# Feed-forward of a hybrid decoder trunk: unit 4 of six becomes a unit of seven block products, so that three such units follow each other

## The chip, the cores and the metric

The kernel runs on one core of one Trainium2 chip. Its time is the device time of one execution in microseconds (us); lower is better. TensorE (PE in the profile) multiplies, VectorE (DVE) and ScalarE (ACT) work element by element, GpSimd (POOL) here issues a few DMAs and small operations, SyncE (SP) issues the plain DMAs.

## What is computed

A trunk of four layers over 256 tokens of width 1024. Each layer is a feed-forward, a token mixer (attention, SSD, short convolution, attention in turn) and a second feed-forward; so there are eight feed-forwards. The change touches these alone:

```python
def swiglu(x, w_gu, w_down):          # x 256 x 1024, w_gu 1024 x 5632, w_down 2816 x 1024
    gate, up = jnp.split(x @ w_gu, 2, axis=-1)
    return (jax.nn.silu(gate) * up) @ w_down

for i in range(DEPTH):                # DEPTH = 4
    x = x + 0.5 * swiglu(rmsnorm(x, ffn1_norm[i]), ffn1_w_gu[i], ffn1_w_down[i])
    x = x + mixer_i(rmsnorm(x, mix_norm[i]))
    x = x + 0.5 * swiglu(rmsnorm(x, ffn2_norm[i]), ffn2_w_gu[i], ffn2_w_down[i])
```

## The kernel before

**Weights.** All weights are float32 and pass through the core once. A weight block is 512 x 512 (or 256 x 1024) numbers, 1 MB, as a tile of 128 x 2048. It is loaded by DMA into one of six staging slots (`stage`; slots 3 to 5 lie in the `arena`, so their rows show that name), then split in two: ScalarE copies it, rounded, into `w_hi` (line 721), VectorE subtracts that from the block and writes the rest into `w_lo` (line 1067). There are three pairs of `w_hi` and `w_lo`, used in turn: ScalarE may fill a pair once TensorE has ended the block three before. TensorE then makes each product in three passes, high by high, high by low and low by high, with matmuls of 512 columns.

**Units.** A feed-forward goes over the 2816 hidden columns in six units, u = 0 to 5, whose kinds the string `UNITS` (line 51) gives. A plain unit `P` takes 512 hidden columns, that is four weight blocks, G0, G1 (gate) and U0, U1 (up), each multiplied with both halves of the tokens: 24 matmuls a block, 96 in all, in banks 4, 5 and 6, 7. `H` is a plain unit of 256 columns with two blocks, H0 and H1. `S` also takes 512 columns, but by the scheme of seven products: gate, up, the two halves of the 1024 inputs and the two halves of the tokens make a 2 x 2 by 2 x 2 block product, which needs seven block products instead of eight when sums of blocks are multiplied. They are B11, A1, B22, A3, B21, A2, A4, each with 12 matmuls (line 1633), 84 in all. B blocks come as they are loaded; A blocks are sums of weight blocks:

- A1: VectorE adds block B12 to B11 in B11's slot (`weight_sum`, line 1178). It does so before ScalarE can split A1.
- A3: GpSimd issues an accumulating DMA that adds B22 to B12's slot (line 660), once the sum for A1 is done.
- A2: a second accumulating DMA adds B22 to B11's slot (line 663), once A1's low part is done.
- A4: VectorE adds that slot to B21's (line 1178), once the second DMA has landed.

The results of the products overlap in banks 4 to 7, and gate and up come out of them by sums: ScalarE copies three banks to SBUF (line 784), VectorE makes five part sums (line 1151), ScalarE the silu of two (line 780) and VectorE the product with up (line 1147). TensorE transposes the hidden into banks 6 and 7 (line 1667), which are split into `mt_hi` (ScalarE, line 790) and `mt_lo` (VectorE, line 1157). Then come the down blocks of the unit, D0 and D1, 24 matmuls each (line 1520).

**Order.** `ffn_order` writes out the order of all blocks of a feed-forward; `DOWNS` says how many waiting down blocks go into each unit. Before the change it is, with the unit's number: 0: G0 G1 U0 U1. 1: B11 A1 B22 D0(0) D1(0) A3 B21 A2 A4. 2: H0 H1 D0(1). 3: B11 A1 D1(1) B22 D0(2) A3 B21 A2 A4. 4: G0 G1 D0(3) U0 U1 D1(3). 5: B11 A1 B22 D0(4) A3 B21 A2 A4 D1(4) D0(5) D1(5). A unit's transposes follow the first two products, or the first block, of the next.

Every engine works its own list in order, made from this one. ScalarE and VectorE split the block that is two ahead: at step i they do first what TensorE's block i-1 released (copies, part sums), then the split of block i+2, and where block i+2 is B11, VectorE then makes the sum for A1; where it is B21, the sum for A4. Before the first block of a unit that follows an `S` unit, TensorE waits until bank 4 is copied and the third part sum has read bank 5:

```python
                    else:
                        pe.wait_ge(part_copied, 3 * sums_before(f, u))
                        pe.wait_ge(part_summed, 5 * sums_before(f, u) - 2)
```

Loads are issued by SyncE in order, each as soon as the slot's last user is split; a planner gives each load the slot that is free first.

Of the kernel before, what the change touches and what calls it, by code (L numbers as in the profile page):

```python
# [47 lines left out]
SSD_STAGE_SLOTS = 3  # L48


UNITS = "PSHSPS"
DOWNS = (0, 2, 1, 2, 2, 1)


def unit_col(u):

    return sum(256 if kind == "H" else 512 for kind in UNITS[:u])


def down_parts(u):  # L60

    return 1 if UNITS[u] == "H" else 2


def ffn_order():

    order, turned, waiting = [], {}, []
    for u, kind in enumerate(UNITS):
        own = {"P": ("G0", "G1", "U0", "U1"), "H": ("H0", "H1"),
               "S": ("B11", "A1", "B22", "A3", "B21", "A2", "A4")}[kind]  # L70
        own = [(u, name) for name in own]
        lead, head = {"P": (1, 2), "H": (1, 2), "S": (2, 3)}[kind]
        if u:
            waiting += [(u - 1, f"D{j}") for j in range(down_parts(u - 1))]
        now, waiting = waiting[:DOWNS[u]], waiting[DOWNS[u]:]
        order += own[:lead]
        if u:
            turned[u - 1] = len(order) - 1
        if kind == "S" and UNITS[u - 1] == "H":
            order += now[:1]  # L80
            now = now[1:]
        order += own[lead:head]
        if kind == "P":
            order += now[:1] + own[2:] + now[1:]
        else:
            order += now + own[head:]
    turned[u] = len(order) - 1
    return order + waiting + [(u, f"D{j}") for j in range(down_parts(u))], turned


FFN_ORDER, TURNED_AFTER = ffn_order()
N_UNITS, N_SUMS = len(UNITS), UNITS.count("S")
HOME = {"A1": "B11", "A2": "B11", "A3": "B12", "A4": "B21"}
# [13 lines left out]
def build_trunk(nc, x, ffn1_norm, ffn1_w_gu, ffn1_w_down, mix_norm, ffn2_norm, ffn2_w_gu,  # L107
# [149 lines left out]
    def sums_before(f, u):  # L257

        return N_SUMS * f + UNITS[:u].count("S")

# [1842 lines left out]
```

## Time and profile before

| | |
|---|---|
| median of 3 runs | 2031.96 us (2031.28 to 2492.7) |
| profiled execution | 2032.11 us, span of its instructions 2030.4 us |
| TensorE busy | 2000.0 us, 99% of the span, 10299 matmuls |
| VectorE busy | 1566.5 us, 77% |
| ScalarE busy | 1185.2 us, 58% |
| GpSimd busy | 166.4 us, 8% |
| DMA | 419.87 MB, mean 207 GB/s |
| granted TensorE clock | 0.999 |

The busy times are of one profiled execution. A matmul's own duration (0.39 us for 512 columns) overlaps the next one's; what a block takes is read from start to start. The feed-forward that is looked at most closely is the third of eight (the first of layer 1), at about 504 to 684 us.

### The profile page before, as it was taken

What the parts mean: (1) busy time and instruction counts of PE and PEld (TensorE: products, weight loads), DVE (VectorE), ACT (ScalarE), POOL (GpSimd) and SP (SyncE); (2) the same over time, 40 slices, a digit from 0 to 9 for tenths busy, and PEclk for the clock granted to TensorE, in tenths of its full rate; (3) what the DMA queues carried; (4) which work ended last, traced back from release to release, by engine and by line L of the source; (5) the groups of instructions that cost most, each with busy time, mean ns of one, the idle gap of its engine ahead of it and who ended that gap; (6) DMA issues with size and microseconds to landing.
All of it is one profiled execution on the core that took longest, in us unless ns stands there. A gap on an engine that the chain in (4) does not pass through costs nothing.

```text
span 2030.4 us, 25272 instructions
## 1 busy us (share of the span) xinstructions
PE 2000.0 (99%) x10299; PEld 1705.7 (84%) x10299; DVE 1566.5 (77%) x1485; ACT 1185.2 (58%) x1263; POOL 166.4 (8%) x164
## 2 busy tenths in 40 slices
PE   7999999999999999999999999999999999999998
PEld 6888997888888889988888888988888888998886
DVE  6778577878887879968878778778778778567776
ACT  6556576556665666756556556446555546576544
POOL 1000001000000014410001000000001001001000
PEclk9999999999999999999999999999999999999999
DMA  8867534877787485368876867658876867534863
GB/s 268 254 230 228 185 104 129 246 247 228 224 251 210 138 263 141 125 226 237 243 218 192 250 231 194 204 190 247 243 227 190 256 214 232 166 121 129 260 223 108
DMA packets 242183, 419.87 MB, mean 207 GB/s; under 512 B 10668, under 2 KB 92932, under 8 KB 241556
## 3 DMA queue, kind: packets, MB, share of 16 engines
q1 hardware_dynamic: 216020, 363.65, 52.9%
q0 software_dynamic: 26048, 54.61, 14.9%
q8 instruction: 82, 1.34, 0.3%
q14 instruction: 33, 0.27, 0.0%
HBM read 417.14 MB, written 1.08 MB: 206 GB/s over the span
## 4 chain that ended last, share of the span: by engine, by line
PE 87%; DVE 7%; ACT 3%; issue 1%; DMA 1%; POOL 0%; SPq 0%; DVEq 0%; POOLq 0%; ACTq 0%
PE bank L1520 51%; PE bank L1633 22%; PE bank L1526 7%; DVE w_lo L1067 3%; PE bank L1667 2%; DVE arena L1387 2%; ACT w_hi L721 2%; PE bank L1553 1%; PE bank L1804 1%; PE bank L1835 1%; DMA stage<-in_ffn_w_gu 0%; PE bank L1817 0%; ACT arena L965 0%; DMA arena<-seg_rows 0%; DVE arena L1427 0%
## 5 line engine op out<-in xcount | busy, mean ns | idle before, releaser
L1067 DVE TENSOR_TENSOR w_lo<-stage,w_hi 128x2048 fp32r<-128x2048 f32 (+1 forms) x225 | 517.0, 2299 | 161.4 <-ACT w_hi L721 160.2
L1067 DVE TENSOR_TENSOR w_lo<-arena,w_hi 128x2048 fp32r<-128x2048 f32 (+1 forms) x196 | 444.3, 2267 | 167.5 <-ACT w_hi L721 166.7
L721 ACT ACTIVATE w_hi<-stage 128x2048 fp32r<-128x2048 f32 (+1 forms) x225 | 425.4, 1892 | 216.6 <-PE bank L1520 143.0
L721 ACT ACTIVATE w_hi<-arena 128x2048 fp32r<-128x2048 f32 (+1 forms) x196 | 371.9, 1898 | 241.3 <-PE bank L1520 160.0
L1520 PE MATMUL bank<-w_hi,mt_hi 128*128 128x512 f32 x928 | 367.4, 396 | 5.2 <-DVE mt_lo L1274 3.8
L1520 PE MATMUL bank<-w_lo,mt_hi 128*128 128x512 f32 x928 | 361.5, 390 | 0.0
L1520 PE MATMUL bank<-w_hi,mt_lo 128*128 128x512 f32 x928 | 360.9, 390 | 0.0
L1520 PE MATMUL bank<-w_hi,xt_hi 128*128 128x512 f32 x704 | 279.7, 397 | 2.1 <-DVE w_lo L1067 1.6
L1520 PE MATMUL bank<-w_lo,xt_hi 128*128 128x512 f32 x704 | 275.7, 392 | 0.0
L1520 PE MATMUL bank<-w_hi,xt_lo 128*128 128x512 f32 x704 | 251.7, 390 | 0.0
L1520 PEld LDWEIGHTS bank<-w_hi,mt_hi 128*128 128x128 f32 x928 | 174.4, 188 | 40.3 <-DVE mt_lo L1274 4.2
L1520 PEld LDWEIGHTS bank<-w_hi,mt_lo 128*128 128x128 f32 x928 | 174.2, 188 | 37.0
L1526 PE MATMUL bank<-xt_hi,w_hi 128*128 128x256 f32 x704 | 203.4, 290 | 1.2 <-DVE arena L1387 0.7
L1520 PEld LDWEIGHTS bank<-w_lo,mt_hi 128*128 128x128 f32 x928 | 174.5, 188 | 34.4
L1526 PE MATMUL bank<-xt_hi,w_lo 128*128 128x256 f32 x704 | 198.1, 283 | 0.0
L1526 PE MATMUL bank<-xt_lo,w_hi 128*128 128x256 f32 x704 | 195.4, 283 | 0.0
L1520 PEld LDWEIGHTS bank<-w_hi,xt_hi 128*128 128x128 f32 x704 | 132.9, 189 | 32.5 <-issue 3.9
L1520 PEld LDWEIGHTS bank<-w_hi,xt_lo 128*128 128x128 f32 x704 | 132.2, 188 | 28.0
L1520 PEld LDWEIGHTS bank<-w_lo,xt_hi 128*128 128x128 f32 x704 | 132.9, 189 | 26.2
L1633 PE MATMUL bank<-w_hi,mt_hi 128*128 128x512 f32 x384 | 151.1, 393 | 0.1
L1633 PE MATMUL bank<-w_hi,mt_lo 128*128 128x512 f32 x384 | 149.7, 390 | 0.0
L1633 PE MATMUL bank<-w_lo,mt_hi 128*128 128x512 f32 x384 | 149.5, 389 | 0.0
(213 smaller groups left out, 2802.8 us busy)
## 6 DMA issues: line engine op xcount, KB each, us to landing
arena<-in_ffn_w_gu SPq DMA_DIRECT2D x81, 1024.0 KB, 5.3
stage<-in_ffn_w_gu SPq DMA_DIRECT2D x79, 1024.0 KB, 5.2
stage<-in_ffn_w_down SPq DMA_DIRECT2D x96, 512.0 KB, 4.9
arena<-in_ffn_w_down SPq DMA_DIRECT2D x80, 512.0 KB, 4.9
arena<-in_ffn_w_gu POOLq DMA_DIRECT2D x29, 1024.0 KB, 9.8
stage<-in_ffn_w_gu POOLq DMA_DIRECT2D x19, 1024.0 KB, 9.8
stage<-in_ffn_w_gu SPq DMA_DIRECT2D x18, 512.0 KB, 8.8
stage<-in_sb_w_qkv SPq DMA_DIRECT2D x16, 512.0 KB, 4.6
```

The costliest lines, as they stand in the source:

```text
L721: act.activation(w_hi[q][:, 0:c], stage[s][:, 0:c], ACT.Copy).then_inc(hi_done, 1)
L1067: dve.tensor_tensor(w_lo[q][:, 0:c], stage[s][:, 0:c], w_hi[q][:, 0:c].bitcast(F32), ALU.subtract).then_inc(lo_done, 1)
L1387: dve.scalar_tensor_tensor(chan[:, c, i:SEQ], bank[c][:, 0:SEQ - i], par[:, t:t + 1], chan[:, c, i:SEQ], ALU.mult, ALU.add).then_inc(tap_d ...
L1520: mm = pe.matmul(out_, x_[a], w[b], start=start and (a, b) == (0, 0), stop=stop and (a, b) == (1, 0))
L1526: mm = pe.matmul(out_, w[b], x_[a], start=start and (a, b) == (0, 0), stop=stop and (a, b) == (1, 0), skip_group_check=True)
L1553: mm = pe.transpose(tb[i % 2][:, k * P:(k + 1) * P], xk, ident[:, :])
L1633: mm = pe.matmul(out_[:, :], x[a], w[b], start=start and k == 0 and (a, b) == (0, 0), stop=stop and k == 3 and (a, b) == (1, 0), skip_grou ...
L1667: mm = pe.transpose(tb[b][:, c * SEQ + h * P:c * SEQ + (h + 1) * P], hid[:, h, col:col + P], ident[:, :])
L1804: pe.matmul(z[:, 0:SEQ], kk[:, 0:P], qq, start=True, stop=True, skip_group_check=True)
L1835: pe.matmul(o[:, 0:SEQ], v(0), w[:, 0:SEQ], start=h % 2 == 0, stop=True, skip_group_check=True)
```

## The change

The string of the units gets an `S` in the place of its last `P`. Unit 4 is then one of seven products, and units 3, 4 and 5 are all of this kind.

```diff
--- before.py
+++ after.py
@@ -48,7 +48,7 @@
 SSD_STAGE_SLOTS = 3
 
 
-UNITS = "PSHSPS"
+UNITS = "PSHSSS"
 DOWNS = (0, 2, 1, 2, 2, 1)
```

The order of blocks in units 4 and 5 becomes: 4: B11 A1 B22 D0(3) D1(3) A3 B21 A2 A4. 5: as before. A feed-forward has 45 steps instead of 42; TensorE has 96 matmuls fewer over the whole program.

Below are VectorE's rows of the first feed-forward where unit 3 ends and unit 4 begins, from the part sum after A3 of unit 3 (line 1151, reading bank 6) on. Line 1067 is the low part of a weight block, line 1178 a weight sum. Before the change:

```order
L1151 TENSOR_TENSOR arena<-arena,bank 128x512 [waits part_copied,block_used]
L1067 TENSOR_TENSOR w_lo<-stage,w_hi 128x2048 [waits hi_done]
L1151 TENSOR_TENSOR arena<-bank,arena 128x512 [waits part_copied,block_used]
L1067 TENSOR_TENSOR w_lo<-arena,w_hi 128x2048 [waits hi_done]
L1151 TENSOR_TENSOR arena<-bank,arena 128x512 [waits part_copied]
L1151 TENSOR_TENSOR arena<-arena 128x512 [waits part_copied,part_summed]
L1067 TENSOR_TENSOR w_lo<-stage,w_hi 128x2048 [waits hi_done]
L1151 TENSOR_TENSOR arena<-bank,arena 128x512 [waits part_copied,block_used]
L1147 TENSOR_TENSOR arena<-arena 128x512 [waits part_summed,silu_done] x2
```

And after it:

```order
L1151 TENSOR_TENSOR arena<-arena,bank 128x512 [waits part_copied,block_used]
L1067 TENSOR_TENSOR w_lo<-stage,w_hi 128x2048 [waits hi_done]
L1151 TENSOR_TENSOR arena<-bank,arena 128x512 [waits part_copied,block_used]
L1067 TENSOR_TENSOR w_lo<-arena,w_hi 128x2048 [waits hi_done]
L1178 TENSOR_TENSOR arena<-stage,arena 128x2048 [waits stage_in0]
L1151 TENSOR_TENSOR arena<-bank,arena 128x512 [waits part_copied]
L1151 TENSOR_TENSOR arena<-arena 128x512 [waits part_copied,part_summed]
L1067 TENSOR_TENSOR w_lo<-arena,w_hi 128x2048 [waits hi_done]
L1151 TENSOR_TENSOR arena<-bank,arena 128x512 [waits part_copied,block_used]
L1147 TENSOR_TENSOR arena<-arena 128x512 [waits part_summed,silu_done] x2
```

The low part behind the second row of line 1151 is that of unit 4's first block (G0 before, B11 now). Behind it now stands the weight sum for A1 of unit 4, and only then the two part sums that follow A2 of unit 3, the first of which frees bank 5.

ScalarE's rows at the same place, from the high part of A4 of unit 3 on (line 721, waiting for w_summed), before:

```order
L721 ACTIVATE w_hi<-stage 128x2048 [waits block_used,w_summed]
L721 ACTIVATE w_hi<-arena 128x2048 [waits block_used,stage_in3]
L784 ACTIVATE arena<-bank 128x512 [waits block_used]
L721 ACTIVATE w_hi<-stage 128x2048 [waits block_used,stage_in0]
L780 ACTIVATE arena<-arena,rstd 128x512 [waits part_summed] x2
L721 ACTIVATE w_hi<-stage 128x2048 [waits block_used,stage_in1]
L790 ACTIVATE mt_hi<-bank 128x512 [waits ht_ps] x2
L721 ACTIVATE w_hi<-arena 128x2048 [waits block_used,stage_in4]
```

and after:

```order
L721 ACTIVATE w_hi<-stage 128x2048 [waits block_used,w_summed]
L721 ACTIVATE w_hi<-arena 128x2048 [waits block_used,stage_in3]
L784 ACTIVATE arena<-bank 128x512 [waits block_used]
L721 ACTIVATE w_hi<-arena 128x2048 [waits block_used,w_summed]
L780 ACTIVATE arena<-arena,rstd 128x512 [waits part_summed] x2
L721 ACTIVATE w_hi<-stage 128x2048 [waits block_used,stage_in1]
L784 ACTIVATE arena<-bank 128x512 [waits block_used]
L721 ACTIVATE w_hi<-arena 128x2048 [waits block_used,stage_in4]
L784 ACTIVATE arena<-bank 128x512 [waits block_used]
L790 ACTIVATE mt_hi<-bank 128x512 [waits ht_ps] x2
```

The second block of unit 4 (the row ahead of line 780) waited for its load and now waits for a weight sum, and the copies of line 784 for unit 4 stand between the high parts.

On TensorE the first matmul of unit 4 keeps its waits: for its low part, for the copy of bank 4 and for the third part sum of unit 3. It is now a product's matmul (line 1633), and 12 of them stand before the next block, where there were 24.

## Rows read from the trace of the kernel before

**Rows 1.** Page: engines' busy time, share and count; the chain that ended last

```profile
PE 2000.0 (99%) x10299; PEld 1705.7 (84%) x10299; DVE 1566.5 (77%) x1485; ACT 1185.2 (58%) x1263; POOL 166.4 (8%) x164
...
PE 87%; DVE 7%; ACT 3%; issue 1%; DMA 1%; POOL 0%; SPq 0%; DVEq 0%; POOLq 0%; ACTq 0%
```

**Rows 2.** Windows: length, busy us of PE, PEld, DVE, ACT, POOL; clock, DMA share, GB/s

```profile
605.60:648.50 42.90, 42.90 (x197) 35.53 (x197) 28.74 (x21) 22.42 (x19) 2.56 (x2) 1.00 0.75 208
```

**Rows 3.** TensorE's waits, whole run: total us, times, longest

```profile
PE bank L1520 <- DVE mt_lo L1274: 3.8, 2, 1.9
...
PE bank L1520 <- DVE w_lo L1067: 1.6, 1, 1.6
```

**Rows 4.** Timeline of VectorE: start, us, line, operation; end of unit 3

```profile
602.54 2.28 DVE L1067 TENSOR_TENSOR w_lo<-stage,w_hi 128x2048 fp32r<-128x2048 f32 x1
604.74 0.68 DVE L1151 TENSOR_TENSOR arena<-bank,arena 128x512 f32<-128x512 f32 x1
605.35 0.68 DVE L1151 TENSOR_TENSOR arena<-arena 128x512 f32<-128x512 f32 x1
```

**Rows 5.** Timeline of TensorE where unit 4 begins

```profile
605.61 0.44 PE L1520 MATMUL bank<-w_hi,xt_hi 128*128 128x512 f32 x1
```

**Rows 6.** Timeline of TensorE, unit 5: B11, A1, transposes, B22, D0(4), A3

```profile
639.28 0.39 PE L1633 MATMUL bank<-w_hi,xt_hi 128*128 128x512 f32 x1
...
642.00 0.39 PE L1633 MATMUL bank<-w_hi,mt_hi 128*128 128x512 f32 x1
...
644.72 1.03 PE L1667 MATMUL bank<-ident,arena 128*128 128x128 f32 x8
645.66 0.47 PE L1633 MATMUL bank<-w_hi,mt_hi 128*128 128x512 f32 x1
...
648.50 0.39 PE L1520 MATMUL bank<-w_hi,mt_hi 128*128 128x512 f32 x1
...
653.95 0.39 PE L1633 MATMUL bank<-w_hi,mt_hi 128*128 128x512 f32 x1
```

**Rows 7.** Timeline of all engines where TensorE waits for VectorE in attention

```profile
306.57 0.41 DVE L1274 TENSOR_TENSOR mt_lo<-bank,mt_hi 128x256 fp32r<-128x256 f32 x1
...
307.04 0.50 PE L1520 MATMUL bank<-w_hi,mt_hi 128*128 128x512 f32 x1 [1.91 <-DVE mt_lo L1274]
...
307.38 0.39 PE L1520 MATMUL bank<-w_lo,mt_hi 128*128 128x512 f32 x1
...
307.61 0.40 PE L1520 MATMUL bank<-w_hi,mt_lo 128*128 128x512 f32 x1
```

**Rows 8.** Timeline of all engines, A1 of unit 5: sum, high part, low part

```profile
632.82 2.29 DVE L1178 TENSOR_TENSOR stage<-stage 128x2048 f32<-128x2048 f32 x1
...
635.13 1.92 ACT L721 ACTIVATE w_hi<-stage 128x2048 fp32r<-128x2048 f32 x1 [4.56 <-DVE stage L1178]
635.39 1.28 POOL L660 DMA_DIRECT2D stage<-in_ffn_w_gu  x1 [57.82 <-DVE stage L1178]
637.09 2.29 DVE L1067 TENSOR_TENSOR w_lo<-stage,w_hi 128x2048 fp32r<-128x2048 f32 x1 [0.79 <-ACT w_hi L721]
```

**Rows 9.** Accumulating DMAs by line, from issue to landing: line 663, then line 660

```profile
DMA to landing us min/median/max: 9.7/10.5/13.2
...
DMA to landing us min/median/max: 8.5/8.7/9.8
```

**Rows 10.** Page: DMA queues, packets, MB, share of 16 engines

```profile
q1 hardware_dynamic: 216020, 363.65, 52.9%
q0 software_dynamic: 26048, 54.61, 14.9%
```

**Rows 11.** Timeline of TensorE in the first microseconds

```profile
12.71 1.11 PE L1553 MATMUL bank<-ident,x_res 128*128 128x128 f32 x4 [4.47 <-DMA x_res<-in_x]
...
16.43 0.63 PE L1520 MATMUL bank<-w_hi,xt_hi 128*128 128x512 f32 x1
16.86 0.63 PE L1520 MATMUL bank<-w_lo,xt_hi 128*128 128x512 f32 x1
```

## The prediction

> **What bounds the kernel now.** First the page's busy shares and its chain [rows 1]: TensorE is busy 99% of the span, VectorE 77%, and TensorE's own matmuls make 87% of the chain that ended last. The kernel is bound by TensorE nearly everywhere, so matmuls removed are worth their full price, provided that the feeders still arrive in time. The windows view [rows 2] shows that for the stretch that the change rewrites, in the third of eight feed-forwards: from 605.6 to 648.5 us TensorE is busy 42.90 of 42.90 us, VectorE 28.74, ScalarE 22.42, the DMA engines 75%. TensorE's waits [rows 3] hold one wait on a low part (w_lo) in the whole run, 1.6 us, at the start; no feed-forward stalls on its weights.
>
> Averages don't say how late the feeders are. For that I read VectorE's and ScalarE's timelines beside TensorE's, at the one place where a unit of seven products ends (unit 3; the units are numbered 0 to 5 as in the code). There the covers are thin. The third part sum of unit 3 runs 604.74 to 605.42 [rows 4], and the next unit's first matmul, which waits for it, starts at 605.61 [rows 5]: 0.19 us between them, with TensorE never idle. That wait is what the change meets.
>
> **What the change takes away.** Unit 4 turns from four blocks of 24 matmuls into seven of 12: 84 for 96. A product takes 2.72 us (639.28, 642.00, 644.72 [rows 6]), a down block 5.45 (648.50 to 653.95 [rows 6]). Today the stretch from unit 4's first matmul, 605.61, to the down block D0(4), 648.50, takes 42.89 us. Afterwards it holds, without any stall: B11, A1, transposes and B22 of unit 4, for which the same pieces of unit 5 stand, 648.50 - 639.28 = 9.22; two down blocks, 10.90; A3, B21, A2, A4, 4 x 2.72 = 10.88; and the 9.22 of unit 5. That is 40.22, so 2.67 us less in each feed-forward. With eight of them 21.4 us.
>
> **What it adds.** VectorE: three more low parts and two more weight sums, each 2.20 us from start to start (602.54 to 604.74), five part sums of 0.60 [rows 4], while ScalarE gets three more high parts and three copies for the two silus that it keeps. On average that fits: 5 x 2.20 + 5 x 0.60 = 14.0 us on top of 28.74 is 42.7, but of a stretch that now lasts 40.2 to 47 us. So VectorE goes from a third idle to nearly full, and what counts is the order in which it works. The order shows the new trouble: between the low part of unit 4's first block and the third part sum of unit 3 now stands the 2048-wide weight sum for A1 of unit 4. I carry the times forward from the rows, with t as in the trace.
>
> *First stall, B11.* VectorE starts the weight sum at 604.74, where the third part sum stood, and goes on 2.20 us later, at 606.94. The part sum ends 0.68 later, at 607.62. TensorE reacts to a VectorE result in 0.06 us (low part of mt ends 306.57 + 0.41 = 306.98, matmul at 307.04 [rows 7]), so B11 starts at 607.68: **2.07 us late**. Nothing hides it, since bank 4 and bank 5 still hold unit 3's results.
>
> *Second stall, A1.* Its weights exist only once summed: sum, then high part, then low part, in a chain. Today's A1 of unit 5 shows the links: sum 632.82 + 2.29, high part at 635.13, low part at 637.09 [rows 8]. There two blocks of 5.4 us stood ahead of B11 and TensorE reached A1 only at 642.00. In the new place: sum ends 604.74 + 2.29 = 607.03, high part 607.05 to 608.97, low part 609.01 to 611.30, TensorE 611.36. B11 ends at 607.68 + 2.72 + 0.12 = 610.52 (0.12: after a wait the first matmul takes 0.34 to the next instead of 0.23 [rows 7]). **0.84 us late**. Even without the first stall A1 would wait for this chain.
>
> *Third, B22.* After A1's low part is issued (611.22) VectorE has a part sum and two products of the hidden, 1.80 us, then B22's low part, 613.02 to 615.31, TensorE 615.37. TensorE would be there at 611.36 + 2.84 + 0.94 (transposes, 644.72 to 645.66) = 615.14. **0.23 us late**, B22 ends at 618.21. The low half of the hidden is ready at 615.23 + 2.21 + 0.68 = 618.12, so D0(3) does not wait. It would start at 605.61 + 9.22 = 614.83 without stalls: the transition costs **3.38 us**.
>
> *Again at unit 5.* The two down blocks (10.90 us) let VectorE catch up: it has two low parts, one more and a sum in them. So A3 to A4 of unit 4 run at the same margins as unit 3's, and the transition from 4 to 5 costs the same 3.38. This also delays the second added DMA of unit 5, whose issue follows A1's low part by 0.3 us: 645.7 + 0.3 = 646.0; with the median of 10.5 us to landing [rows 9] it is there by 656.5, and the sum for A4 may start as late as 658.9 before A2's low part misses TensorE at 663.5. The slots of the staging area are freed six or seven blocks ahead in the new order, as now, so the plain loads keep their lead.
>
> *Sum.* 2 x 3.38 - 2.67 = +4.09 us per feed-forward; eight times, **+32.7 us**. Outside the feed-forwards nothing changes but slot numbers. The profiled execution took 2032.11 us (span 2030.4), the median shown is 2031.96. So 2064.7, rounded to 2065 us, 1.6% slower.
>
> **Prices seen from one side only.** A stall's restart (0.12) may not be paid where it falls before a wait that VectorE sets anyway; it may be paid three more times per transition: 0 to +0.36 each, 0 to +6 us. Bank 4's part sum might be read with 0.19 instead of 0.06 us of delay: 0 to +2. The extra DMA traffic: the accumulating queue moved 54.61 MB in 14.9% of the span and the other 363.65 MB in 52.9% [rows 10], so the eight new units add 16 MB at 5.5 us per MB, 92 us of DMA time in all, hidden in a DMA that is 75% busy here, and free unless a landing comes late.
>
> **Rivals.**
> *The second added DMA lands too late.* 24 of them took 9.7 to 13.2 us [rows 9]; unit 5's limit is 658.9 - 646.0 = 12.9. At 14 to 15 each feed-forward loses 1 to 2 us more: 2073 to 2081. For it: it runs beside denser traffic and a denser VectorE. Against it: the same loads surround it today, and only the slowest exceeds the limit. The Trainium skill (SBUF: State Buffer, "SBUF: two separate sides") says that GpSimd's descriptors wait while VectorE works in a two-port mode. By that rule each issue could be late by one VectorE instruction, 2.3 us, which is 13.2 to landing and +0.3 us per feed-forward; the trace shows the first added DMA issued at 635.39 right behind a weight sum and beside further VectorE work [rows 8], and all 24 of its kind landed within 8.5 to 9.8 us [rows 9], a spread of 1.3. Chance 0.10.
>
> *TensorE's clock falls in the stalls.* The granted clock is 1.00 in this stretch [rows 2], the 2.4 GHz level. When TensorE had been idle 4.47 us at the start, its matmuls then came 0.43 us apart rather than 0.23 [rows 11], the 1.2 GHz level. The new stalls are 2.1 and 0.8 us. If each transition lost one product's time to it, 16 x 2.72 = 43 us: 2108. Against it: after 1.91 us of idle at 307.04 the spacing is 0.23 at once [rows 7]. The Trainium skill (TensorE: Matmul & The Clock Gate, "What's actually happening") has the same two levels and says that inactivity brings the lower one; by it, stalls that add up would cost this way. Chance 0.05.
>
> *No stalls: it is faster.* If the transitions hid their waits, 2032.1 - 21.4 = 2011. The averages speak for it (VectorE 77%), and it decides at 1.34 us per transition: under that the change gains. Against it stands the order: 2.20 us of sum before a wait with 0.19 us of slack. Chance 0.05.
>
> *Half of it.* The second and third stall vanish, because B11's stall gives the feeders time: 2 x 2.07 - 2.67 = 1.47, 2044. I computed them behind the first, so I give it 0.08.
>
> **The numbers.** The forecast, 2058 to 2072 on its own, has 0.72. With a late landing and part of the half case the range that leaves out 2 in 10 is 2050 to 2080. Two per cent, about what a measurement of this kernel can tell, is 41 us: slower means over 2072.6. That takes the late landing, the clock and a little of the forecast's upper end: 0.17. Faster by over 2% would be below 1991, which only a mechanism I don't see gives: 0.01. Within 2%: 0.82.
>
> **What would show it.** TensorE's matmul count falls by 96 and its waits on a part sum (line 1151) appear 16 times at about 2.1 us, waits on w_lo (line 1067) 32 times at 0.8 and 0.2; TensorE's busy time falls by 22 us while the span grows. The weight sum (line 1178) stands right before the third part sum. Wrong would be: stalls at A3 to A4 of unit 5 (the landing), matmuls 0.43 apart, a total wait per transition under 1.3 us, or stalls in the first three units, which the change leaves alone.

## The result and the profile after

| | before | after |
|---|---|---|
| median, us | 2032.04 (4 runs) | 2071.66 (2070.94 to 2073.1, 4 runs) |
| ratio to before | | 1.0197 (95%: 1.0181 to 1.0213) |
| span of the profiled execution, us | 2030.4 | 2069.2 |
| matmuls | 10299 | 10203 |
| granted clock | 0.999 | 0.992 |

The changed kernel is 39.6 us slower. Forecast were 2065 us and +33, in a range of 2050 to 2080. The ratio is one of mean times and leaves out one run before of 2492.7 us.

The page of the changed kernel, engines' busy time, then the chain that ended last:

```profile
PE 2000.8 (97%) x10203; PEld 1695.2 (82%) x10203; DVE 1675.1 (81%) x1565; ACT 1243.3 (60%) x1311; POOL 186.8 (9%) x180
...
PE 74%; DVE 14%; ACT 5%; issue 5%; DMA 1%; POOL 0%; SPq 0%; DVEq 0%; POOLq 0%; ACTq 0%
```

Against [rows 1], TensorE has 96 matmuls less and VectorE 109 us more. TensorE's part of the chain went from 87 to 74%, and VectorE's doubled: at some places the feeders now set the pace. TensorE's busy time did not fall by the 21 us that the matmuls taken away were worth. In a feed-forward without a fall of the clock it fell by 1.0 to 1.1 us, not by 2.67 (178.11 for 179.17 us in the second), since the waits break up its stream; the falls, below, put the rest back (178.88 for 178.87 in the third). TensorE's waits in the changed kernel (total us, times, longest) say where:

```profile
PE bank L1633 <- DVE arena L1151: 32.2, 16, 2.0
...
PE bank L1633 <- DVE w_lo L1067: 5.3, 9, 0.6
```

Neither row was there before [rows 3]. The first counts 16 waits on a part sum, two in each of eight feed-forwards; the second is A1's wait at nine of these 16 places. VectorE's timeline of the changed kernel at the second of them in the third feed-forward, start and duration in us:

```profile
646.30 2.28 DVE L1067 TENSOR_TENSOR w_lo<-stage,w_hi 128x2048 fp32r<-128x2048 f32 x1
648.50 2.29 DVE L1178 TENSOR_TENSOR stage<-stage 128x2048 f32<-128x2048 f32 x1
650.70 0.69 DVE L1151 TENSOR_TENSOR arena<-bank,arena 128x512 f32<-128x512 f32 x1
651.30 0.68 DVE L1151 TENSOR_TENSOR arena<-arena 128x512 f32<-128x512 f32 x1
652.76 2.29 DVE L1067 TENSOR_TENSOR w_lo<-stage,w_hi 128x2048 fp32r<-128x2048 f32 x1 [0.78 <-ACT w_hi L721]
```

and TensorE's there, the first matmuls of B11, of A1, and of the down block behind B22:

```profile
651.53 0.47 PE L1633 MATMUL bank<-w_hi,xt_hi 128*128 128x512 f32 x1 [2.01 <-DVE arena L1151]
...
655.11 0.50 PE L1633 MATMUL bank<-w_hi,mt_hi 128*128 128x512 f32 x1 [0.57 <-DVE w_lo L1067]
...
662.01 0.47 PE L1520 MATMUL bank<-w_hi,mt_hi 128*128 128x512 f32 x1
```

The weight sum stands between the low part of B11 and the part sum. That part sum ends at 651.39 and B11 starts 0.14 us later. The block ahead ended at 649.35 (its first matmul at 646.63, plus 2.72), so B11 is 2.18 us late. From 649.35 to the down block at 662.01 the meeting (the place where one unit of seven products follows another) takes 12.66 us where [rows 6] had 9.22: it costs **3.44 us**.

What the waits don't show is the clock. Windows over the two meetings of the same feed-forward (length, busy us of PE, PEld, DVE, ACT, POOL, then granted clock, DMA share and GB/s):

```profile
614.00:628.00 14.00, 11.99 (x49) 9.40 (x48) 13.22 (x12) 10.87 (x11) 2.55 (x2) 0.88 0.87 169
649.00:662.00 13.00, 10.30 (x47) 7.57 (x46) 12.22 (x11) 10.73 (x10) 2.56 (x2) 1.00 0.84 161
```

In the first of them the granted clock fell, right behind the idle 2.01 us; TensorE's timeline shows the matmuls of B11 getting 0.43 us apart instead of 0.23:

```profile
616.64 0.47 PE L1633 MATMUL bank<-w_hi,xt_hi 128*128 128x512 f32 x1 [2.01 <-DVE arena L1151]
...
617.74 0.63 PE L1633 MATMUL bank<-w_hi,xt_hi 128*128 128x512 f32 x1
618.16 0.63 PE L1633 MATMUL bank<-w_lo,xt_hi 128*128 128x512 f32 x1
```

That is the 1.2 GHz level. It happened at 7 of the 16 meetings of the profiled execution. Such a meeting takes 13.07 to 13.13 us (here 614.47 to 627.60), 0.42 to 0.48 more than the other kind, and not more because A1 would have waited for its weights anyway.

**Where the 38.8 us of span went.** From the first transposes of one entry to those of the next, the eight feed-forwards take 4.33 to 5.06 us more each, 37.1 in all. Those without a fall of the clock take 4.33 to 4.40 more: 2 x 3.44 - 2.67 = 4.21, and 0.09 at the down block behind each meeting (5.53 to 5.56 us where 5.45 were needed before). Eight times 4.37 is 35.0. The other 2.1 us are what the seven falls add, about 0.35 each (0.42 to 0.48, less the 0.09 that the down block behind them does not lose), less a first feed-forward that waited 0.6 us less for its input. Of the 1.7 us outside the feed-forwards 1.6 stand in the last attention, where the clock fell behind an idle 1.91 us that the kernel before has too, in its profile without a fall.

### The profile page after: what moved, and what is told of

Read it like the earlier page. It is cut to its first block, busy times and chain, and to the rows that moved or that the text cites. A ratio compares the mean times of both kernels' runs of the same rounds, so it can differ in the third digit from the quotient of the medians.

```text
span 2069.2 us, 25288 instructions
## 1 busy us (share of the span) xinstructions
PE 2000.8 (97%) x10203; PEld 1695.2 (82%) x10203; DVE 1675.1 (81%) x1565; ACT 1243.3 (60%) x1311; POOL 186.8 (9%) x180
## 2 busy tenths in 40 slices
DMA packets 250632, 436.65 MB, mean 211 GB/s; under 512 B 10924, under 2 KB 93188, under 8 KB 250004
## 4 chain that ended last, share of the span: by engine, by line
PE 74%; DVE 14%; ACT 5%; issue 5%; DMA 1%; POOL 0%; SPq 0%; DVEq 0%; POOLq 0%; ACTq 0%
PE bank L1520 42%; PE bank L1633 19%; PE bank L1526 7%; DVE w_lo L1067 7%; ACT w_hi L721 4%; DVE arena L1387 2%; PE bank L1667 1%; DVE arena L1151 1%; DVE stage L1178 1%; DVE arena L1178 1%; PE bank L1553 1%; PE bank L1804 1%; PE bank L1835 1%; PE bank L1817 0%; DMA stage<-in_ffn_w_gu 0%
## 5 line engine op out<-in xcount | busy, mean ns | idle before, releaser
L1067 DVE TENSOR_TENSOR w_lo<-stage,w_hi 128x2048 fp32r<-128x2048 f32 (+1 forms) x241 | 553.4, 2299 | 134.2 <-ACT w_hi L721 133.3
L721 ACT ACTIVATE w_hi<-stage 128x2048 fp32r<-128x2048 f32 (+1 forms) x241 | 456.1, 1893 | 267.2 <-PE bank L1520 159.1
L1067 DVE TENSOR_TENSOR w_lo<-arena,w_hi 128x2048 fp32r<-128x2048 f32 (+1 forms) x204 | 462.2, 2267 | 124.7 <-ACT w_hi L721 124.1
L721 ACT ACTIVATE w_hi<-arena 128x2048 fp32r<-128x2048 f32 (+1 forms) x204 | 387.2, 1898 | 217.7 <-PE bank L1520 136.5
L1520 PE MATMUL bank<-w_hi,mt_hi 128*128 128x512 f32 x928 | 368.6, 397 | 5.6 <-DVE mt_lo L1274 3.8
L1520 PE MATMUL bank<-w_lo,mt_hi 128*128 128x512 f32 x928 | 362.2, 390 | 0.0
L1520 PE MATMUL bank<-w_hi,mt_lo 128*128 128x512 f32 x928 | 361.7, 391 | 0.0
L1633 PE MATMUL bank<-w_hi,mt_hi 128*128 128x512 f32 x512 | 203.0, 396 | 6.4 <-DVE w_lo L1067 5.3
L1633 PE MATMUL bank<-w_hi,mt_lo 128*128 128x512 f32 x512 | 199.6, 390 | 0.0
L1633 PE MATMUL bank<-w_lo,mt_hi 128*128 128x512 f32 x512 | 199.5, 390 | 0.0
L1633 PE MATMUL bank<-w_hi,xt_hi 128*128 128x512 f32 x384 | 154.9, 403 | 32.2 <-DVE arena L1151 32.2
L1520 PE MATMUL bank<-w_hi,xt_hi 128*128 128x512 f32 x448 | 179.1, 400 | 2.1 <-DVE w_lo L1067 1.6
L1520 PE MATMUL bank<-w_lo,xt_hi 128*128 128x512 f32 x448 | 175.8, 392 | 0.0
L1633 PE MATMUL bank<-w_lo,xt_hi 128*128 128x512 f32 x384 | 154.3, 402 | 0.0
L1633 PE MATMUL bank<-w_hi,xt_lo 128*128 128x512 f32 x384 | 153.9, 401 | 0.0
L1520 PE MATMUL bank<-w_hi,xt_lo 128*128 128x512 f32 x448 | 151.9, 390 | 0.0
```

The source lines that it names most:

```text
L721: act.activation(w_hi[q][:, 0:c], stage[s][:, 0:c], ACT.Copy).then_inc(hi_done, 1)
L1067: dve.tensor_tensor(w_lo[q][:, 0:c], stage[s][:, 0:c], w_hi[q][:, 0:c].bitcast(F32), ALU.subtract).then_inc(lo_done, 1)
L1520: mm = pe.matmul(out_, x_[a], w[b], start=start and (a, b) == (0, 0), stop=stop and (a, b) == (1, 0))
L1633: mm = pe.matmul(out_[:, :], x[a], w[b], start=start and k == 0 and (a, b) == (0, 0), stop=stop and k == 3 and (a, b) == (1, 0), skip_grou ...
```

## The experiments

Each kernel ran on the chip together with the kernel before, and differences are to the median of the kernel before in those runs: 2033.3 us for the first four, 2032.9 for the next three, 2031.2 for the eighth and ninth, 2034.0 for the last. Two theories stood at the start. The *chain theory*: at a meeting A1's weights exist only after sum, high part and low part, 6.5 us in a row, and B11's wait is its first symptom. The *saturation theory*: VectorE and the DMAs are too full over three such units, wherever the sum stands.

### The sum behind the part sums

```diff
                         part_sum(u, sg[:, 1, :], p57, p16, 3, ALU.subtract)
+                        if u + 1 < N_UNITS and UNITS[u + 1] == "S":
+                            weight_sum(u + 1, "A1")
...
-                        if name == "B11":
+                        if name == "B11" and UNITS[u - 1] != "S":
                             weight_sum(u, "A1")
```

> The changed kernel, but between two units of seven products VectorE makes the weight sum for A1 behind the two part sums that follow A2, not ahead of them. Theory (the chain sum, high part, low part of A1 is the bound of the transition, and the wait of B11 only its first symptom): the 16 waits of 2.0 us on a part sum vanish, and A1 waits instead. The sum starts two part sums later, 1.2 us; A1's low part ends at 611.30 + 1.21 = 612.5 on the clock of the profile of before, B11 ends at 608.33, so A1 waits 4.2 us, and a transition costs 3.4 + 1.2 = 4.6 us: 2032 + 16 x 4.6 - 21.4 = 2084 us. Rival (the misplaced sum is the whole loss, A1's chain hides behind the rest): waits of B11 vanish, A1 waits 0.6 us, 2032 + 16 x 1.2 - 21.4 = 2030 us.

Measured: 2111.23 us (2 runs), +78. TensorE's waits in this kernel:

```profile
PE bank L1635 <- DVE w_lo L1067: 63.8, 16, 4.0
```

All 16 waits moved from the part sum to A1's low part, and doubled to 4.0 us idle. So the sum in its old place is not a slip that could simply be undone: two part sums ahead of the chain cost more than they give. Of 78 us 52 were forecast. What goes beyond is the clock's, which fell at all 16 meetings. A window over one of them shows 0.74 of full clock:

```profile
125.00:135.00 10.00, 10.00 (x37) 7.98 (x38) 8.51 (x8) 6.96 (x8) 1.28 (x1) 0.74 1.12 219
```

Here the fall comes around A1's wait, and nothing behind it hides what it costs. From A1's start to the down block TensorE needs 6.50 us at full clock [rows 6] and 0.12 for the restart; here the same 32 matmuls take 8.10 to 9.35 us, 8.57 on average. That is 1.95 us a meeting, 31 in all. The profiled span grew by 77.7 us, so with the 21.4 saved a meeting costs 6.2 us: 1.95 for the clock and 4.2 for the stall itself, where 4.6 were forecast.

### A down block between B11 and A1

```diff
-DOWNS = (0, 2, 1, 2, 2, 1)
+DOWNS = (0, 1, 1, 2, 2, 2)
...
-        order += own[:lead]
+        if kind == "S" and UNITS[u - 1] == "S":
+            order += own[:1] + now[:1] + own[1:lead]
+            now = now[1:]
+        else:
+            order += own[:lead]
```

> The changed kernel with a down block of 5.45 us moved between B11 and A1 wherever two units of seven products meet; one down block less in unit 1. The sum for A1 stays ahead of the part sums. Theory: B11's wait on the part sum stays at 2.0 us idle (2.17 late), A1's and B22's vanish, since A1's low part has 5.45 us more: 2032 + 16 x 2.2 - 21.4 = 2046 us. Rival (A1's weights are late by themselves, or unit 1, with one down block less, or its second accumulating DMA now stalls): 2055 us or more, with waits of A1, or of A3 to A4 in unit 1.

Measured: 2061.85 us (2 runs), +28.6, and one kind of wait left:

```profile
PE bank L1637 <- DVE arena L1155: 32.2, 16, 2.0
```

The waits came out as forecast, the time 16 us higher. Feed-forwards in which the clock did not fall take 1.91 to 2.01 us more than before, and 2 x (2.17 + 0.12) - 2.67 = 1.91. The second, with one fall, takes 3.50 more and those with two take 5.05 to 5.09. So a fall costs **1.6 us** where no other wait hides it, and it fell at 8 of 16 meetings: 13 us, and once more in attention. A window shows it:

```profile
608.40:614.40 6.00, 5.93 (x19) 4.75 (x20) 6.00 (x6) 4.62 (x5) 0.90 (x1) 0.72 0.78 128
```

### The down block between, and the sum later

```diff
-                        if name == "B11":
+                        if name == "B11" and UNITS[u - 1] != "S":
                             weight_sum(u, "A1")
+                        elif name[0] == "D" and FFN_ORDER[i + 1][1] == "B11":
+                            weight_sum(FFN_ORDER[i + 1][0], "A1")
```

(on top of the kernel before this one, with the sum's old place left to units that follow a plain one)

> As the kernel with the down block between, and the sum for A1 made behind the part sums and behind that down block's low part. Theory: B11 no longer waits. The sum starts at about 608.2 on the clock of before, A1's low part ends near 614.7, and TensorE would be there at 605.61 + 2.72 + 5.45 = 613.8: about 1 us late. 2032 + 16 x 1.1 - 21.4 = 2028 us, the first version below 2032. Rival (seven products in a row feed too slowly whatever the order, since VectorE is nearly full there): waits move to B22 or to A3 to A4 of units 4 and 5, 2040 us or more.

Measured: 2054.9 us (4 runs), +1.04% (0.87 to 1.21). The expectation of 2028 was wrong. At the meetings it held nearly: A1 waited 0.71 to 0.76 us idle, but at 6 of the 16 B11 still waited up to 0.5 us on the part sum. The larger miss was a new wait in unit 5. Timelines of this kernel, all engines, around it; the accumulating DMA (line 667), the plain loads of SyncE behind it, and the weight sum for A4 (line 1182):

```profile
645.45 1.28 POOL L667 DMA_DIRECT2D stage<-in_ffn_w_gu  x1 [3.00 <-DVE w_lo L1071]
647.47 0.80 SPq L565 DMA_DIRECT2D arena<-in_ffn_w_down  x2
649.67 0.88 SPq L565 DMA_DIRECT2D stage<-in_ffn_w_down  x2
660.41 2.29 DVE L1182 TENSOR_TENSOR arena<-arena,stage 128x2048 f32<-128x2048 f32 x1 [3.94 <-DMA stage<-in_ffn_w_gu]
```

The DMA needed 14.9 us to land, VectorE stood idle 3.94 us for it, and TensorE then waited 2.06 us at A2. Over the eight feed-forwards this wait is 0.97 to 2.09 us, 11.9 in all, and behind two of the three that are over 1.9 us the clock fell. In the eight units 5 this landing took 13.6 to 14.9 us, against 10.7 to 11.6 in the changed kernel. This is the prediction's rival of the late landing, with its limit of 12.9 us; the change itself stayed under it, this order did not.

### One meeting instead of two

```diff
-UNITS = "PSHSSS"
+UNITS = "PSHPSS"
```

> Units P S H P S S: three units of seven products as before the change, 96 matmuls more than the changed kernel, but one pair of them meets. This is the price of a meeting alone. Theory: one transition of 3.4 us per feed-forward and no saving: 2032 + 8 x 3.4 to 3.8 (where the clock falls) = 2059 to 2063 us, with 8 waits of 2.0 us on the part sum. Rival (the loss comes from the number of sums and from the DMA traffic, not from the meeting): within 5 us of 2032.

Measured: 2062.79 us (2 runs), +29.5. Eight waits on the part sum, 16.1 us idle together. With three units of seven products, as many sums, matmuls and bytes as before, one meeting costs 3.6 us per feed-forward without a fall of the clock and 3.9 to 4.0 with one. The saturation theory, which wanted this kernel near 2032, has lost its main support.

### The sum cut short

```diff
+                    if name == "A1" and UNITS[u - 1] == "S":
+                        to, a, b = to[:, 0:64], a[:, 0:64], b[:, 0:64]
+                        dve.wait_ge(lo_done, b0 + FFN_ORDER.index((u, "B11")) + 1)
                     dve.tensor_tensor(to, a, b, ALU.add).then_inc(w_summed, 1)
```

> The changed kernel, but where two units of seven products meet the weight sum for A1 covers 64 of its 2048 columns (the rest of A1 is left unsummed, so the output is not the reference's); instructions, order and DMAs stay. Theory (the length of this sum is what makes B11 late, and the chain behind it A1): the sum is done in 0.2 us instead of 2.2, so B11 is late by 0.3 at most. A1's high part can start at about 605.1 on the clock of the profile of before, low part to 609.3, TensorE at 608.4: late by 0.8 to 1.0; B22 by 0.3 to 0.5. A meeting costs about 1.5 us instead of 3.4: 2032 + 16 x 1.5 - 21.4 = 2035 us. Rival (a nearly full VectorE, or the added DMA traffic, slows the units whatever the sum's length): 2055 us or more.

Measured: 2038.74 us (8 runs), +0.30% (0.20 to 0.40). Order, number of instructions and DMA traffic are those of the changed kernel, and about 34 of its 39.6 us are gone. TensorE idles 0.14 us at B11 now, which is 0.30 late (a part of it is the wait for B11's low part that the edit adds ahead of the short sum), and A1's waits are left:

```profile
PE bank L1636 <- DVE w_lo L1067: 9.5, 16, 0.6
```

The clock did not fall at any of the 16 meetings. One thing this run leaves open: the cut takes 32 us of work off VectorE too (1642.9 us busy for 1675.1), so by itself it does not tell a shorter chain from a less full VectorE. The last kernel below, with the whole sum, does.

### Covers moved further back

```diff
-DOWNS = (0, 1, 1, 2, 2, 2)
+DOWNS = (0, 1, 1, 1, 2, 3)
```

> As the kernel with the down block between B11 and A1 and the later sum, with the down blocks shifted back by one more: unit 3 gets one, unit 4 two, unit 5 three, so that two stand between B22 and A3 of unit 5. Theory (what kept that kernel at 2055 was the second accumulating DMA of unit 5, 13.6 to 14.9 us to landing, for which A2 waited up to 2 us and which a second down block covers; and 0.9 us at A1): 2032 + 16 x 1.1 - 21.4 = 2028 us, plus up to 1.7 us for each fall of the clock, 2028 to 2036. Rival (the covers were only moved: unit 3 or 4, now with one block less, waits for its own accumulating DMA): 2045 us or more, waits on w_lo at A3 to A4 there.

Measured: 2050.93 us (4 runs), +0.86% (0.69 to 1.02). The rival was right: unit 5's waits are gone, with landings as long as before (13.8 to 15.0 us), but unit 3, with one down block less, waits 0.64 us on VectorE and the meeting behind it 0.4 to 0.5.

> The down blocks as in the kernel before this one, and the weight sum for A1 at the meetings cut to 64 of 2048 columns and in its old place ahead of the part sums (output not the reference's). This measures the saving itself, with every wait covered. Theory (12 matmuls fewer per feed-forward are worth 2.67 us each time): 2032 - 21.4 = 2011 us, with at most 0.3 us at each B11, so 2011 to 2016. Rival (TensorE cannot use the saving, since VectorE is full over the last three units): above 2025 us.

The same order with the sum cut to 64 columns: 2032.26 us (8 runs), ratio 0.9992 (0.9981 to 1.0002), not 2011. Without a sum for A1 to blame, TensorE still waits 0.64 us at A2 of unit 3 and 0.81 us at B11 behind it. That looks like saturation, but the timelines of this kernel show a chain again. The high part of B21, then VectorE from A3's low part to A2's, and TensorE at A2:

```profile
580.06 1.92 ACT L725 ACTIVATE w_hi<-arena 128x2048 fp32r<-128x2048 f32 x1 [3.09 <-PE bank L1527]
...
577.01 2.29 DVE L1071 TENSOR_TENSOR w_lo<-stage,w_hi 128x2048 fp32r<-128x2048 f32 x1 [0.32 <-ACT w_hi L725]
582.01 2.29 DVE L1071 TENSOR_TENSOR w_lo<-arena,w_hi 128x2048 fp32r<-128x2048 f32 x1 [2.71 <-ACT w_hi L725]
584.22 2.28 DVE L1185 TENSOR_TENSOR arena<-arena,stage 128x2048 f32<-128x2048 f32 x1
586.43 2.28 DVE L1071 TENSOR_TENSOR w_lo<-stage,w_hi 128x2048 fp32r<-128x2048 f32 x1
...
588.77 0.50 PE L1640 MATMUL bank<-w_hi,mt_hi 128*128 128x512 f32 x1 [0.64 <-DVE w_lo L1071]
```

VectorE had been idle for 2.71 us. It waited for B21's high part, and ScalarE for the pair of `w_hi` and `w_lo` that the block three before, the down block D0(1), held until about 580. From there high part, low part, the sum for A4 and A2's low part take 8.7 us in a row, while TensorE has only B22, A3 and B21 ahead of A2, 3 x 2.72 = 8.16 us. With a down block between B22 and A3 it is B22 that holds the pair, and TensorE has 5.45 + 2 x 2.72 = 10.9 us from its end to A2. From 582.01 to 595.24 VectorE then works with no idle time over 0.2 us, which is how the delay reaches the part sum that B11 waits for. The expectation of 2011 us missed this, since it counted unit 3 as covered.

### Unit 3's cover kept, the sum cut

The kernel with the down block between (`DOWNS` 0, 1, 1, 2, 2, 2) and the cut sum ahead of the part sums.

> The kernel with a down block between B11 and A1 (unit 3 keeps its two down blocks, unit 5 has one behind B22), with the weight sum for A1 at the meetings cut to 64 of 2048 columns in its old place (output not the reference's). Same question as the one before it, whose unit 3 had lost a down block and waited 0.6 and 0.8 us on VectorE there. Theory (with unit 3's cover kept and the sum out of the way, TensorE can use the 2.67 us per feed-forward): 2032 - 21.4 = 2011 us plus at most 0.3 at each B11, 2011 to 2017. Rival (VectorE is full over units 3 to 5 whatever the order): 2025 us or more.

Measured: 2019.16 us (2 runs), ratio 0.9939 (0.9919 to 0.9959). TensorE has no wait on a part sum or on a feed-forward's low part over 0.14 us, and a feed-forward without disturbance takes 1.8 us less than before. That is -2.67 + 2 x 0.42, where 0.42 is B11's remaining lateness (0.30) and its restart (0.12). So 1.8 of the 2.67 us show as time; that the rest is there too is worked out from B11's lateness, not measured.

### Loads held back until the DMA has landed

```diff
                 if name in ("D0", "D1"):
+                    if name == "D0" and u == N_UNITS - 1:
+                        sp.wait_ge(a2_in, 16 * (sums_before(nth("ffn", p), u) + 1))
```

(on the kernel of 2054.9 us)

> The kernel with the down block between and the later sum (2055 us), and SyncE now waits for the landing of unit 5's second accumulating DMA before it issues the load of unit 5's first down block. Theory (the plain loads issued 2 us behind that DMA stretch its landing from 10.9 to 13.6 to 14.9 us, and the sum for A4 waits for it): landing at 11 us or less, the waits of up to 2.1 us at A2 of unit 5 gone, about 2.2 us less per feed-forward: 2032 to 2042 us. Rival (the landing is long because of the accumulating DMA's own descriptors beside a denser VectorE): landing stays above 13 us and the time at 2055 us.

Measured: 2034.28 us (10 runs), ratio 1.0013 (1.0003 to 1.0022). The second accumulating DMA of unit 5 now lands in 9.2 to 10.7 us, in place of 13.6 to 14.9. The plain loads, 2 us behind it, had stretched it. This one wait on SyncE's queue, which holds up loads that nobody needs yet, gave about 19 us: +3.0 to the kernel before, where it was +21.6. At A1 of the 16 meetings TensorE waits as before, 0.71 to 0.75 us.

### The sum ahead of the fourth part sum

On that kernel, at the meetings:

```diff
-                    if name == "A2":
+                    if name == ("A4" if meets(u) else "A2"):
                         silu_summed(u, 0)
                         silu_summed(u, 1)
...
                             weight_sum(FFN_ORDER[i + 1][0], "A1")
+                            fourth_part(FFN_ORDER[i + 1][0] - 1)
+                        elif name == "A1" and meets(u - 1):
+                            hidden_summed(u - 1, 0)
+                            hidden_summed(u - 1, 1)
```

> The kernel with the down block between, the later sum and the loads held back (2034 us), and at the meetings VectorE makes the sum for A1 ahead of the fourth part sum, and A1's low part ahead of the two products of the hidden; ScalarE makes A1's high part ahead of the two silus. Theory (A1 waits 0.7 us because two operations stand ahead of its chain): the sum starts one part sum (0.60 us) earlier, A1's wait falls from 0.74 to about 0.2 us, 16 x 0.5 = 8 us less: 2026 us, the first version with the full output that is faster than before. Rival (the time is only passed on: the hidden comes later, and the transposes or B22 behind A1 wait instead): 2034 us, with waits on the hidden (line 1160) or on w_lo at B22.

Measured: **2023.52 us** (5 runs), ratio to the kernel before **0.9949** (0.9935 to 0.9962), with the full computation. VectorE's timeline of this kernel at a meeting: low part of the down block, sum, fourth and fifth part sums, A1's low part, the products of the hidden:

```profile
599.33 2.29 DVE L1080 TENSOR_TENSOR w_lo<-stage,w_hi 128x2048 fp32r<-128x2048 f32 x1
601.54 2.28 DVE L1196 TENSOR_TENSOR stage<-arena,stage 128x2048 f32<-128x2048 f32 x1
603.75 0.68 DVE L1164 TENSOR_TENSOR arena<-arena 128x512 f32<-128x512 f32 x1
604.35 0.68 DVE L1164 TENSOR_TENSOR arena<-bank,arena 128x512 f32<-128x512 f32 x1
605.81 2.29 DVE L1080 TENSOR_TENSOR w_lo<-stage,w_hi 128x2048 fp32r<-128x2048 f32 x1 [0.78 <-ACT w_hi L734]
608.02 1.29 DVE L1160 TENSOR_TENSOR arena<-arena 128x512 f32<-128x512 f32 x2
```

and TensorE's wait on the low part in all:

```profile
PE bank L1658 <- DVE w_lo L1080: 5.0, 15, 0.4
```

A1 waits 0.31 to 0.37 us at 15 meetings in place of 0.71 to 0.75 at 16, and B11 waits at one meeting instead of five; in the profiles the eight feed-forwards are 9 us shorter together than in the kernel before this one. From +3.0 to -10.5 the medians went down by 13.6 us, more than the 8 forecast; the 4 to 5 us beyond the feed-forwards' 9 were not followed up.

This kernel also settles what the cut sums left open. Its page:

```profile
PE 1988.4 (98%) x10203; PEld 1688.8 (83%) x10203; DVE 1675.9 (83%) x1565; ACT 1241.0 (61%) x1311; POOL 186.7 (9%) x180
```

VectorE has the work of the changed kernel (1675.1 us, 1565 instructions), and the DMAs move the same 436.65 MB, yet the span is 2024.1 us instead of 2069.2. What those 45 us hung on was the order of the work and the time at which loads were issued, not how full VectorE or the DMAs were. The saturation theory is out.

## Why the prediction was right, point by point

- **The saving, 2.67 us per feed-forward.** Held: it enters every account above. With the waits covered 1.8 us of it show as time (2019 us), and B11's remaining lateness accounts for the other 0.84. What did not hold is the sign named for it, TensorE's busy time 22 us lower: it rose by 0.8.
- **First stall, B11, 2.07 us late.** Measured 2.17 to 2.18 at each of the 16 meetings. The 0.1 is the way from VectorE's part sum to TensorE's start, 0.14 instead of 0.06 us; the step had it as a bound up to 0.19.
- **Second and third stall, 0.84 and 0.23 us.** Idle 0.60 and 0.10 by the record. By the starts A1 comes 3.58 us behind B11, 0.74 beyond 2.84, and B22 1.12 to 1.15 us behind the transposes' start where 0.94 was counted, 0.2 late. What they lack to the forecast went into the first stall.
- **The transition, 3.38 us, twice.** Measured 3.44 where the clock did not fall, and the second at the same price. The waits on w_lo were forecast 32 times at 0.8 and 0.2 us; the record has 9, at 0.6, since behind a fall A1 no longer waits and B22's wait is mostly 0.1.
- **The late landing.** It did not happen in the changed kernel (10.7 to 11.6 us, limit 12.9), but another order brought it (13.6 to 14.9 us), and there it cost about 19 us. The reason given for it was half right. Not VectorE's density, the plain loads beside it stretch the landing: holding the loads back, with VectorE's work as it was, brought it from 14 to 9.5 us. The Trainium skill (SBUF: State Buffer, "SBUF: two separate sides") describes VectorE holding up the descriptors of GpSimd's DMAs while it works in a two-port mode. The prediction applied this to VectorE's work here, and that was a misreading: the rows of VectorE shown are all tensor_tensor, and the same page of the Trainium skill ("Who interferes with whom") says that tensor_tensor has no such mode.
- **The clock.** This is the step that was mis-sized. The prediction took a yes or no: no fall, since after 1.91 us at 307.04 there was none, or 2.7 us at each meeting, 43 in all. In truth the clock fell at some meetings with an idle of 2 us and not at others, 7 of 16, and of the 1.6 us that a fall costs elsewhere A1's wait hid all but 0.42 to 0.48 there. So "matmuls 0.43 apart", which the prediction had named as a sign of being wrong, did appear. With the fall in attention (1.6) the clock makes 3.7 of the 6.1 us by which the span went beyond the forecast of +32.7. One row with no fall after 1.91 us was no proof that none would follow the next, and [rows 11], read as a fall after 4.47 us, show none: TensorE ran at the lower level before that idle too, since its first eight transposes took 1.97 us at 6.28 us and the eight in [rows 6] 1.03. The Trainium skill (TensorE: Matmul & The Clock Gate, "What's actually happening") has inactivity bring the lower level; the runs agree in direction.
- **The rest**, 2.4 us: at each of the 16 meetings 0.06 in the transition and 0.09 in a restart at the down block behind it (662.01 to 667.57, 5.56 against 5.45), by the feed-forwards without a fall. The prediction had priced both kinds from one side.
- **No stalls, or half of them.** Not seen.

That the time still lies inside 2058 to 2072, the range of the forecast on its own, is in part luck: the 3.7 us of the clock were no term of it, and the room above was kept for restarts that came to less.

The chances put 0.82 on "within 2%". The ratio is 1.0197 (1.0181 to 1.0213), at that border, and the interval crosses it.

## What to carry to other kernels

A mean busy share of 77% hid the bound. What decides is the feeder's list in order at the place where two dense stretches meet: which operation stands ahead of the one waited for, and how long the chain is from there to the next block's weights. A cut in the bound engine's work makes its blocks shorter, and with them every cover that the feeders had; the gain came only after the chain had been given a down block to hide behind (2062), been moved to its best place (2055, 2024) and the DMA it had collided with been freed (2034). Buffers belong to the chain too: with three pairs of parts, the block three before decides when a block's high part can start. Stalls should be counted with the clock: behind 2 us of idle a fall came at 20 of 40 meetings and cost up to 1.6 us more.

## What the hardware showed that was not expected

**The longer TensorE was idle at a meeting, the more often the granted clock fell behind it.** Falls at meetings, by TensorE's longest idle there, one profiled execution each:

| longest idle at a meeting | meetings | with a fall |
|---|---|---|
| 4.0 us (sum behind the part sums) | 16 | 16 |
| 2.0 us (changed kernel; down block between; one meeting) | 16; 16; 8 | 7; 8; 5 |
| 0.7 to 0.8 us (down block between and sum later; covers further back; loads held back) | 16; 16; 16 | 0; 0; 0 |
| 0.6 us (sum cut) | 16 | 0 |
| 0.3 to 0.4 us (last kernel) | 16 | 0 |

It also explains single differences of 1.6 us in attention, behind an idle 1.91 us that every kernel has twice: the clock fell behind 9 of these 24. What else besides the idle time decides whether the clock falls was not tried.

**An accumulating DMA is stretched by plain loads issued behind it.** Landing of the second accumulating DMA of unit 5 (1 MB): 9.2 to 10.7 us with the loads held back, 10.7 to 11.6 with the first loads 3.3 to 3.7 us behind it (655.35 and 659.09 in the changed kernel), 13.6 to 14.9 with two loads 1.6 to 2.4 and two more about 4 us behind it. In the kernels with the cut sum and a down block between, two loads came 1.5 to 2.3 us behind and the next only after 5.5, and it took 11.5 to 14.1 us. Only the difference between 13.6 to 14.9 and 9.2 to 10.7 was made by moving the loads alone. The distance is not all: in the kernel before, with the first loads 3.8 to 4.1 us behind, it took 10.8 to 13.2 us.

```profile
655.35 1.28 POOL L663 DMA_DIRECT2D stage<-in_ffn_w_gu  x1 [3.00 <-DVE w_lo L1067]
...
659.09 3.06 SPq L561 DMA_DIRECT2D arena<-in_ffn_w_down  x4
```
